# Two blocks on one core: sums of adaLN and of the short convolution in PSUM, a narrow norm, and context products of four key tiles laid inside it

## The reference, cut to what matters

```python
# block one
h = rmsnorm(x, norm_g) * (1 + scale) + shift
cv, cg, cs, lx, ls = split(h @ w_in)
v = causal_depthwise_conv(cv * sigmoid(cg), dw_w, dw_b)          # 31 taps
y_conv = (silu(layernorm(v)) @ pw2_w + pw2_b) * silu(cs)
xs = causal_depthwise_conv(lx, sc_w, sc_b)                       # short: 4 taps
r, i = sigmoid(xh @ wr + br), sigmoid(xh @ wi + bi)              # 8 heads of 128
a = exp(-8 * r * softplus(-lam)); bx = sqrt(1 - a * a) * (i * xs)
y_lru = scan(a, bx) * silu(ls)
x = rmsnorm(x + (1 + gate) * (concat(y_conv, y_lru) @ w_out), final_g)
# block two
sh1, sc1, g1, sh2, sc2, g2 = split(silu(c_2) @ ada_w + ada_b)    # same for c_ctx
hx = rmsnorm(x, pre_mix_g) * (1 + sc1) + sh1                     # hc from ctx
q, k, v, o, gates = split(hx @ m_in_w + m_in_b)   # context: k, v, gates are used
x = x + g1 * rmsnorm(mlstm(...) @ m_out_w, post_mix_g)           # then the FFN
```

## Time and profile before

| | us |
|---|---|
| median of three runs | 2415.22 (2413.39 to 2421.04) |
| the profiled execution | 2414.37 |
| its span, first to last instruction | 2412.5 |
| PE busy | 2173.7 (90%) |
| VectorE busy | 1157.0 (48%) |
| ScalarE busy | 765.7 (32%) |
| GpSimd busy | 725.1 (30%) |

### The profile page before, as it was taken

The page is one execution under the profiler, slowest core; times in us unless marked ns, Lnnn a source line. Parts: engine busy times, 40 slices in busy tenths (PEclk is TensorE's granted clock), DMA queues, the critical chain, the costliest instruction groups (busy, mean ns, idle before and its releaser), DMA issues.

```text
span 2412.5 us, 25840 instructions
## 1 busy us (share of the span) xinstructions
PE 2173.7 (90%) x9820; PEld 1792.2 (74%) x9820; DVE 1157.0 (48%) x1049; ACT 765.7 (32%) x874; POOL 725.1 (30%) x320
## 2 busy tenths in 40 slices
PE   3599999998899988999989985969999999999995
PEld 2488777776678766888868974837888888887874
DVE  6799998988541528502305644054222222322124
ACT  2233345455350322211323434233222222312121
POOL 0185835555312350211111114411222122122240
PEclk7799999999999998999989996989999999999997
DMA  8451111211113322336739856121112221223211
GB/s 304 162 154 39 37 55 57 60 60 46 53 53 113 97 70 76 116 108 205 232 94 265 221 158 199 55 84 35 51 44 61 78 78 60 71 61 114 74 57 70
DMA packets 278204, 243.07 MB, mean 101 GB/s; under 512 B 7346, under 2 KB 246547, under 8 KB 278131
## 3 DMA queue, kind: packets, MB, share of 16 engines
q1 hardware_dynamic: 268451, 232.65, 31.4%
q10 hardware_dynamic: 9680, 9.44, 1.2%
HBM read 194.02 MB, written 48.04 MB: 100 GB/s over the span
## 4 chain that ended last, share of the span: by engine, by line
PE 54%; issue 29%; DVE 6%; POOL 4%; DMA 3%; ACT 2%; SPq 0%; ACTq 0%; POOLq 0%; DVEq 0%
PE PS L1341 42%; POOL wl L662 4%; PE PS L1608 1%; PE PS L1600 1%; PE PS L1601 1%; PE PS L1464 1%; DVE SCR L1712 1%; PE PS L1634 1%; PE PS L1363 1%; DMA B<-rows_d 1%; PE PS L1494 1%; DMA B<-in_mod_w 1%; PE PS L1574 1%; DMA SCR<-in_ctx 1%; PE PS L1594 1%
## 5 line engine op out<-in xcount | busy, mean ns | idle before, releaser
L1341 PE MATMUL PS<-XH,wh 128*128 128x512 f32 x2448 | 765.0, 394 | 30.0 <-POOL wl L662 17.9
L662 POOL TENSOR_TENSOR wl<-raw,wh 128x1024 fp32r<-128x1024 f32 (+2 forms) x173 | 414.0, 2393 | 1208.1 <-ACT wh L861 980.7
L1341 PE MATMUL PS<-XH,wl 128*128 128x512 f32 x2448 | 759.9, 392 | 0.0
L1341 PE MATMUL PS<-XL,wh 128*128 128x512 f32 x2448 | 759.8, 392 | 0.0
L1341 PEld LDWEIGHTS PS<-XH,wh 128*128 128x128 f32 x2448 | 461.5, 190 | 134.8 <-issue 16.9
L1341 PEld LDWEIGHTS PS<-XH,wl 128*128 128x128 f32 x2448 | 464.0, 190 | 97.8
L1341 PEld LDWEIGHTS PS<-XL,wh 128*128 128x128 f32 x2448 | 463.0, 189 | 97.5
L1806 DVE SCALAR_TENSOR_TENSOR PS<-B,PJ,PS 128x1022 f32<-128x1022 f32 (+7 forms) x197 | 251.1, 1274 | 7.5
L861 ACT ACTIVATE wh<-raw 128x1024 fp32r<-128x1024 f32 (+1 forms) x116 | 121.1, 1044 | 308.7 <-PE PS L1341 249.5
L2178 DVE SCALAR_TENSOR_TENSOR SCR<-SCR,PV 128x1008 f32<-128x1008 f32 x22 | 28.0, 1271 | 257.8 <-ACT SCR L1277 257.8
L924 ACT ACTIVATE wh<-raw 128x1024 fp32r<-128x1024 f32 (+1 forms) x56 | 54.0, 965 | 254.0 <-PE PS L1341 200.4
(11 more groups left out here) (323 smaller groups left out, 2482.2 us busy)
## 6 DMA issues: line engine op xcount, KB each, us to landing
B<-in_ada_w SPq DMA_DIRECT2D x48, 512.0 KB, 6.0
raw<-in_ffn_up_w SPq DMA_DIRECT2D x44, 512.0 KB, 4.2
raw<-in_w_in SPq DMA_DIRECT2D x40, 512.0 KB, 3.9
raw<-in_m_in_w SPq DMA_DIRECT2D x25, 512.0 KB, 6.4
B<-in_mod_w SPq DMA_DIRECT2D x6, 2048.0 KB, 8.1
raw<-in_w_out SPq DMA_DIRECT2D x16, 512.0 KB, 4.2
B<-proj_d SPq DMA_DIRECT2D x8, 1024.0 KB, 6.4
SCR<-proj_d SPq DMA_DIRECT2D x8, 1024.0 KB, 6.5
```

The source lines that it names most:

```text
L662: tt(wl[slot][:, 0:kc, :], raw[slot][:, 0:kc, :], wh[slot][:, 0:kc, :].bitcast(F32), ALU.subtract).then_inc(lo_done, 1)
L1341: last = mm(ps[:, c:c + step_n], W[:, k, :], Y[:, k, c:c + step_n], start=(seen == 0), stop=(seen == total - 1))
```

## The change

The sums of ada_w now run in PS[2] and PS[3]; only the last step of each writes SBUF. The column sums on PE wait for all of them and come after units 8 and 10 instead of 6 and 10. The short convolution runs in PS[2], its last step writes xs to SBUF. `DVE_HIGH` goes from 5 to 3. The sums of squares of G3 move from GpSimd to VectorE. A new product CX stands between G3 and the gate tile: the context products of the four key tiles, with their own weight units, evacuated to kctx and stored by one DMA; the key tiles later have none, and their weights are loaded twice. The norm uses token sums, small operations, two diagonals, and two spreads of 512-column matmuls.

```diff
...
@@ -197,6 +197,7 @@
+        kctx = b1[:, 2 * ALL:2 * ALL + HQ // P * CTX].rearrange("p (h t) -> p h t", t=CTX)
@@ -273,7 +274,7 @@
-        DVE_HIGH = KD - 3
+        DVE_HIGH = 3
@@ -297,6 +298,7 @@
+        CX = Product(HQ // P)
@@ -488,7 +490,13 @@
-            for t in range(4):
+            for t in range(CX.n):
+                unit(CX.U + t, (CX.U + t) % 2, cols_of(m_in_w, 0, KD, HQ + P * t))
+            for t in range(2):
+                proj_unit(t, t % 2)
+            sp.wait_ge(*at("kctx_sb", CX.n))
+            sp.dma_start(proj_d[HQ:2 * HQ, 0:CTX].rearrange("(h p) t -> p h t", p=P), kctx).then_inc(ev("kctx_out"), 16)
+            for t in range(2, 4):
@@ -502,6 +510,7 @@
+            sp.wait_ge(*at("kctx_out", 16))
@@ -536,7 +545,7 @@
-                proj_store(t, t % 2, t <= Q_TILES + KV_TILES)
+                proj_store(t, t % 2, 2 * Q_TILES < t <= Q_TILES + KV_TILES)
@@ -763,20 +772,8 @@
-            def x1_sums(i, n=2):
-                for s in range(2):
-                    low(G3.U + 1 + 2 * i + s, (G3.U + 1 + s) % 2)
-                    if s == n:
-                        return
-                    pool.wait_ge(*at("sq_ok", 2 * i + s + 1))
-                    pool.wait_ge(*at("ssq_ok", 2 * (2 * i + s) + 2))
-                    tt(T[4], T[4], T[3], ALU.add).then_inc(ev("ssq_ok"), 1)
-                    tt(T[6], T[6], T[5], ALU.add).then_inc(ev("ssq_ok"), 1)
-            x1_sums(0)
-            with pool.Fori(1, KD // 2 - 1) as i:
-                x1_sums(i)
-            x1_sums(KD // 2 - 1, n=1)
+            low_tiles(G3)
+            low_tiles(CX)
@@ -1093,6 +1090,8 @@
+                    if isinstance(i, int) and t == KD - 1:
+                        high_at(CX.U + 1, 0)
@@ -1106,15 +1105,22 @@
-            with act.Fori(1, KD // 2) as i:
+            with act.Fori(1, KD // 2 - 1) as i:
-            high_at(Gx.U, 0)
-            act.wait_ge(*at("n1_ms", 1))
-            f(T[1], T[1], ACT.Sqrt).then_inc(ev("n1_sd2"), 1)
-            act.wait_ge(*at("stat1_ps", 1))
-            f(T[3], PS[2][:], ACT.Sqrt, bias=eps[:]).then_inc(ev("n1_sd1"), 1)
+            x1_squares(KD // 2 - 1)
+            for t in range(CX.n):
+                b = (CX.T + t) % 2
+                act.wait_ge(unit_used, CX.U + t + 3)
+                f(kctx[:, t, :], PS[b][:, 0:CTX], ACT.Identity, bias=pcol("m_in_b", Q_TILES + t)).then_inc(ev("kctx_sb"), 1)
+                act.wait_ge(*at("kctx_sb", t + 1))
+                act.sem_inc(taken[b], 1)
+                high_at(CX.U + t + 2, 0)
+                if t == 1:
+                    act.wait_ge(*at("stat1_ps", 1))
+                    f(small[:, 1, 0:NT], PS[2][:, 0:NT], ACT.Sqrt, bias=eps[:]).then_inc(ev("n1_sd1"), 1)
+                    act.wait_ge(*at("n1_ms", 1))
+                    f(small[:, 1, NT:2 * NT], small[:, 2, NT:2 * NT], ACT.Sqrt).then_inc(ev("n1_sd2"), 1)
@@ -1153,7 +1159,8 @@
-            proj_pairs(Q_TILES + 1, KV_TILES, True)
+            proj_pairs(Q_TILES + 1, Q_TILES)
+            proj_pairs(2 * Q_TILES + 1, KV_TILES - Q_TILES, True)
@@ -1442,7 +1449,7 @@
-                pe.wait_ge(*at("ada_summed", 2 * KD * (h + 1)))
+                pe.wait_ge(*at("ada_summed", 2 * KD * EARLY))
@@ -1467,8 +1474,8 @@
                 tile(U, U % 2, PS[U % 2], taken[U % 2], U // 2)
-                if U in (6, 10):
-                    ada((U - 6) // 4)
+                if U in (8, 10):
+                    ada((U - 8) // 2)
             tile(lx_unit(0), 0, PS[1], taken[1], KD)
@@ -1511,18 +1518,24 @@
-            pe.wait_ge(*at("ssq_ok", 2 * KD))
-            pe.wait_ge(*at("sq_ok", KD))
-            stat(PS[2], T[4], T[3], event="stat1_ps")
-            stat(PS[3], T[6], T[5], event="stat1_ps2")
+            pe.wait_ge(*at("xl_c", KD))
+            for t in range(CX.n):
+                if t == 2:
+                    pe.wait_ge(*at("ssq_ok", 2 * KD))
+                    pe.wait_ge(*at("sq_ok", KD))
+                    for q, srcs in enumerate(((T[4], T[3]), (T[6], T[5]))):
+                        token_sums(PS[2][:, SEQ // 2 * q:SEQ // 2 * q + NT], *srcs, event=("stat1_ps", "stat1_ps2")[q])
+                b = (CX.T + t) % 2
+                tile(CX.U + t, (CX.U + t) % 2, PS[b], taken[b], (CX.T + t) // 2, X=(XCH, XCL), n=CTX)
+            pe.wait_ge(*at("n1_diag", 1))
+            stat(PS[3], T[6], event="n1_r2")
+            pe.wait_ge(*at("n1_diag1", 1))
+            stat(PS[2], T[3], event="n1_r1")
-            pe.wait_ge(*at("xl_c", KD))
-            pe.wait_ge(*at("n1_sd1", 1))
-            pe.wait_ge(*at("n1_ms", 1))
+            pe.wait_ge(*at("n1_copy", 1))
@@ -1770,13 +1784,15 @@
                     dve.wait_ge(*at("side_sum", (SIDE - 1) * (KD - 1)))
+                    dve.wait_ge(*at("ada_sb", 1))
                 else:
                     dve.wait_ge(*at("ixs", i))
-                n = TAPS + 1
-                step.link(V.tensor_scalar(xs_t, lxpad[:, 0:SEQ], PJ[:, i, n:n + 1], PJ[:, i, n + SHORT:n + SHORT + 1], ALU.mult, ALU.add))
+                    dve.wait_ge(*at("r_ok", i))
+                n, acc = TAPS + 1, PS[2][:]
+                step.link(V.tensor_scalar(acc, lxpad[:, 0:SEQ], PJ[:, i, n:n + 1], PJ[:, i, n + SHORT:n + SHORT + 1], ALU.mult, ALU.add))
                 for t in range(1, SHORT):
-                    ins = V.scalar_tensor_tensor(out=xs_t, in0=lxpad[:, t:t + SEQ], scalar=PJ[:, i, n + t:n + t + 1],
-                                                 in1=xs_t, op0=ALU.mult, op1=ALU.add)
+                    ins = V.scalar_tensor_tensor(out=acc if t < SHORT - 1 else xs_t, in0=lxpad[:, t:t + SEQ], scalar=PJ[:, i, n + t:n + t + 1],
+                                                 in1=acc, op0=ALU.mult, op1=ALU.add)
                     if t < SHORT - 1:
@@ -1816,11 +1832,11 @@
-            def add_product(acc, w, k, v):
+            def add_product(acc, w, k, v, out=None):
                     return V.tensor_scalar(acc, w, CA[:, 0, 2 + v:3 + v], None, ALU.mult)
-                return V.scalar_tensor_tensor(out=acc, in0=w, scalar=CA[:, k, 2 + v:3 + v], in1=acc, op0=ALU.mult, op1=ALU.add)
+                return V.scalar_tensor_tensor(out=acc if out is None else out, in0=w, scalar=CA[:, k, 2 + v:3 + v], in1=acc, op0=ALU.mult, op1=ALU.add)
@@ -1828,9 +1844,9 @@
                     for v in range(2):
-                        if k:
+                        if n:
                             dve.wait_ge(*at("ada_summed", 2 * n + v - 1))
-                        add_product(ada_acc[h][v], ada_t[n % 3], k, v).then_inc(ev("ada_summed"), 1)
+                        add_product(PS[2 + v][:], ada_t[n % 3], k, v, ada_acc[h][v] if k == KD - 1 else None).then_inc(ev("ada_summed"), 1)
@@ -1845,6 +1861,7 @@
+            dve.wait_ge(*at("ada_summed", 2 * KD * EARLY))
@@ -1954,7 +1971,14 @@
-            tiles(G3, g3, 1, 0, 1)
+            def x1_sums(t, s, i, ps, tk):
+                g3(t, s, i, ps, tk)
+                dve.wait_ge(*at("sq_ok", t + 1))
+                dve.wait_ge(*at("ssq_ok", 2 * t + 2))
+                V.tensor_tensor(T[4], T[4], T[3], ALU.add).then_inc(ev("ssq_ok"), 1)
+                V.tensor_tensor(T[6], T[6], T[5], ALU.add).then_inc(ev("ssq_ok"), 1)
+            tiles(G3, x1_sums, 1, 0, 1)
@@ -1963,16 +1987,25 @@
-            tiles(G3, g3, 1, 1)
-            dve.wait_ge(*at("stat1_ps", 1))
-            step.link(V.tensor_scalar(T[1], PS[2][:], EPS, EPS, ALU.add, ALU.mult))
+            tiles(G3, x1_sums, 1, 1, KD // 2 - 1)
+            for s in range(2):
+                b = (G3.T + s) % 2
+                dve.wait_ge(unit_used, G3.U + KD + s + 1)
+                (x1_sums if s == 0 else g3)(KD - 2 + s, s, KD // 2 - 1, PS[b], taken[b])
+            dve.wait_ge(*at("n1_sd1", 1))
+            ms2 = small[:, 2, NT:2 * NT]
+            step.link(V.tensor_scalar(ms2, PS[2][:, 0:NT], EPS, EPS, ALU.add, ALU.mult))
-            step.link(V.tensor_tensor(T[1], T[1], PS[3][:], ALU.add))
-            dve.sem_inc(ev("n1_ms"), 1)
+            V.tensor_tensor(ms2, ms2, PS[2][:, SEQ // 2:SEQ // 2 + NT], ALU.add).then_inc(ev("n1_ms"), 1)
-            step.link(V.reciprocal(T[1], T[1]))
+            step.link(V.reciprocal(small[:, 4, 0:2 * NT], small[:, 1, 0:2 * NT]))
+            step.link(V.tensor_scalar(small[:, 3, 0:2 * NT], small[:, 4, 0:2 * NT], float(D), None, ALU.mult))
+            for dst, q, event in ((T[6], 1, "n1_diag"), (T[3], 0, "n1_diag1")):
+                V.tensor_tensor(dst.rearrange("p (c t) -> p c t", t=P), ident[:].rearrange("p (o t) -> p o t", o=1).to_broadcast([P, NT, P]),
+                                bc(small[:, 3, NT * q:NT * (q + 1)], P), ALU.mult).then_inc(ev(event), 1)
+            dve.wait_ge(*at("n1_r2", 1))
@@ -1981,13 +2014,15 @@
-                stt(out=T[4 + k % 2], in0=B2[:, k, :], scalar=SC[:, 5, k:k + 1], in1=T[1], op0=ALU.mult, op1=ALU.mult).then_inc(ev("x2n"), 1)
```

(12 more changed lines are left out.)

6 lines of the change are left out of this document (3 added, 3 removed).

## The result

| | before | after |
|---|---|---|
| median of the runs, us | 2417.03 (4 runs, 2413.39 to 2421.04) | 2375.43 (4 runs, 2372.56 to 2379.65) |
| ratio | | 0.9829, 95% interval 0.9805 to 0.9853 |
| profiled execution, us (span) | 2414.37 (2412.5) | 2377.47 (2375.6) |

Forecast were 2376 and a range of 2361 to 2400. The total came out as forecast; its terms came out in part too large and in part too small, and the errors cancelled. The spans differ by 36.9 us.

What follows compares the result with a forecast made beforehand. TensorE, busy for 90% of the span, was taken as the bound, so only its waits counted. Savings of 22.9 + 0.6 + 7.3 + 8 = 38.8 us from the profiled 2414.37 gave about 2376, range 2361 to 2400.

Steps and rivals of the forecast that it cites:

- What bounds it: Whole kernel: TensorE, busy 90% of the span; savings elsewhere count only where TensorE waits for them.
- gates 1 to 6: Gate products of the recurrent heads: waits go, period 35.6 against 38.0, 14.4 us saved.
- gates 7: Last head's gate products, needing ls evacuated: 4 of the 9.5 us wait saved.
- gates 0: First head's gate products: the 4.5 us wait ahead goes, as VectorE comes earlier.
- Part 1: Short convolution's sum in PSUM: three steps fall from 8.3 to 3.85 us; 22.9 us saved together with gates 0.
- Part 2: adaLN sums in PSUM: VectorE up to 31 us earlier, worth nothing itself but the 4.5 counted at gates 0.
- Part 3: Opening of the output product, three instead of five tiles prepared on VectorE: 0.6 us saved, a wash.
- Part 4: Last product of block one, sums of squares off GpSimd: waits before tiles 4 and 6 go, 7.3 us saved.
- rival F: Slower: collisions between VectorE and GpSimd move, in the heads and the last product; 2432 us, chance 0.05.
- Part 5: Norm between the blocks and key tiles: opening 3 us later, keys 11.6 less, together 8 saved.
- B: Rival: the chain of a head stays the bound, half the heads' waits stay, price 12 to 13; 2389 us, chance 0.14.
- D: Rival, more gain: last head's lru 2.5 us earlier, gates 7 without wait, opening at full clock; 2367 us, chance 0.06.

Runs made afterwards that it cites:

- Experiment 1: Kernel before, with only the short convolution's running sum in PSUM: 2406.68 us, ratio 0.9961.
- experiment 5: Changed kernel; in the tile behind the gates TensorE starts with high-weight products for three chunks, then waits for low weights: 2366.86 us, ratio 0.9797.
- experiment 3: Changed kernel with the adaLN sums back in SBUF and their column sums back behind tiles 6 and 10: 2388.34 us, ratio 0.9889.
- experiment 4: Changed kernel with five instead of three tiles prepared on VectorE ahead of the last scan: 2378.27 us, ratio 0.9844.
- experiment 7: Changed kernel with the sums of squares back on GpSimd: 2383.52 us, ratio 0.9864.
- experiment 8: Changed kernel with the wide norm and the context products of all key tiles as before: 2385.35 us, ratio 0.988.
- experiment 9: Changed kernel with VectorE's second running sum in the last product of block one kept in PSUM: 2373.68 us, ratio 0.982.
- experiment 6: Changed kernel with three chunks of high-weight products before the low-weight wait in every tile but the opening pairs: 2360.84 us, ratio 0.9767.
- experiment 10: On experiment 6, GpSimd's last sum of the long convolution put behind the opening's low parts on VectorE: 2360.51 us, ratio 0.9768.
- experiment 11: On experiment 10, the last head's second gate product moved to the PSUM buffer of cs, and cs to that of ls: 2349.73 us, ratio 0.9723.

## Why the prediction was right, and where it was not

**What bounds it** held: nearly all of the gain was found as waits of PE that went. That the sum came out within 2 us of the trace (38.8 for 36.9) is in part luck: gates 1 to 6 gave 6.1 less than forecast, gates 7 1.2, the opening 1.3 and the last product 1.8 less; gates 0 gave 4.3 more, norm and keys 2.9 more, and 1.4 lie in no term.

**Part 1** was mis-sized, 22.9 with gates 0, of which the trace has 19.8. The durations were right (1.29 forecast as 1.27), and that the gates stop waiting was right. Wrong was the step "the waits of gates 1 to 6 go [...] a period of PE work is 32.7 + 2.9 = 35.6". It counted PE's work and asked whether the chain of the head is shorter; it did not ask for the second resource of a period, the weight buffer. From the end of one tile in a buffer to the next tile in it PE must have at least 0.26 + 1.06 + 0.08 + 2.39, about 3.8 us, of other work, and the gates are 2.88. The question "what is late next" was put for the gates and not for the tile behind them. Experiment 1 shows the wait with this part alone, experiment 5 takes it away and finds the 35.4. The six periods gave 8.3 where 14.4 stood. At gates 7 the wait itself fell by 3.7 (4 forecast), and one 0.96 ahead of it takes the rest.

The wrong term was made up by **gates 0**: 8.8 for 4.5. The mechanism, VectorE held by adaLN sums, is shown by experiment 3. The size was a single wait of one execution, and such a wait is the difference of two arrivals. One of them, PE's, carries half clock behind the column sums, so that the wait is short when PE is slow. What counts is the start of the gates, 323.87, which VectorE sets, against PE's earliest arrival. **Part 2** was called "worth nothing itself but the 4.5": by experiment 3 it is worth some 10 us in the trace, of which 9.0 are this wait, and 14.5 by the times: as much as any other part. Experiment 1 shows the two parts apart: the convolution frees gates 1 to 7, the adaLN sums free gates 0.

**Part 3** was forecast as a wash and is one: -0.7 in the trace, 0.9 the other way round in experiment 4. The one wait is 11.1 (about 10 forecast).

**Part 4**: 5.5 in the trace, 6.8 to 8.5 by experiment 7, for 7.3. Tile 6 no longer waits; tile 4 still waits 2.0, against "the waits go":

```profile
823.54 2.54 POOL L671 TENSOR_TENSOR wl<-raw,wh 128x1024 fp32r<-128x1024 f32 x1 [14.77 <-ACT wh L858]
...
826.21 0.72 PE L1348 MATMUL PS<-XH,wh 128*128 128x512 f32 x2 [2.00 <-POOL wl L671]
```

Its low part ends 23.9 behind the start of tile 2, 0.5 behind the forecast's place, but PE now comes to it after 22.0 instead of 23.65, at the full clock. In experiments 3, 5 and 8, the same product, PE comes after 23.65 as before and waits 0.4, so tile 4 starts 24.0 behind tile 2 in either case. The collisions feared in rival F are there, and they are what is left: VectorE's second addition takes 3.42, and the residual addition, the squares and the high part stand behind it. In experiment 9, where it takes 1.23, this low part starts 20.09 behind tile 2 instead of 21.36, and tile 4 starts without a wait, 23.5 behind:

```profile
820.67 2.59 POOL L671 TENSOR_TENSOR wl<-raw,wh 128x1024 fp32r<-128x1024 f32 x1 [13.51 <-ACT wh L858]
```

**Part 5**: 10.9 for 8. The opening starts 6.0 later behind block one than before, 4 forecast: the token sums took 11.07 for 8.4, and a wait of 1.48 for VectorE's product and copy took the place of the 2.5 that stood for them. Against it stand the keys' 11.6, the opening at the full clock, 1.5 shorter, and 0.6 less of waits behind it: 7.7. The other 3 were in no term; they go with PE's clock. From the opening's end to the gate rows PE is busy 300.95 us before and 286.37 after, 14.6 less for 11.6 less work, at a granted clock of 0.98 for 0.97. The length of this part varies from execution to execution: from the start of the token sums to the gates' context product it is 24.3 here, 22.7 to 22.8 in experiments 3 to 7 and 10, 24.4 in experiment 9 and 26.0 in experiment 11. The first row below is the kernel before, the second the changed one:

```profile
947.95:1261.57 313.62, 300.95 (x1457) 0.97 0.47 153
```
```profile
927.82:1226.04 298.22, 286.37 (x1360) 0.98 0.49 159
```

Of the **rivals** B was the nearest: something of a head does stay the bound, but it is the refill, not the chain, and its price is 6.7 of waits, 7.7 by experiment 5, not 12 to 13. D did not come: gates 7 still wait 5.8. F is excluded: in head 1 GpSimd's two neighbours of the convolution got shorter too, and the scan kept the 2.28 of the earlier trace rows. GpSimd before, then GpSimd and VectorE after:

```profile
344.73 2.85 POOL L662 TENSOR_TENSOR wl<-raw,wh 128x1024 fp32r<-128x1024 f32 x1
...
347.54 3.38 POOL L701 TENSOR_TENSOR SCR<-SCR,B 128x1024 f32<-128x1024 f32 x1
```
```profile
371.18 2.42 POOL L671 TENSOR_TENSOR wl<-raw,wh 128x1024 fp32r<-128x1024 f32 x1
373.53 2.43 POOL L710 TENSOR_TENSOR SCR<-SCR,B 128x1024 f32<-128x1024 f32 x1
```
```profile
375.91 2.28 DVE L1831 TENSOR_TENSOR_SCAN SCR<-SCR 128x1024 f32<-128x1024 f32 x1
```
